# Attention's first unit in a hybrid encoder layer: late powers placed among the convolution's additions on GpSimd, head transposes through two PSUM banks, and TensorE's wait for the cleared row moved to the scores

## What is computed

```python
a = u[..., :C_CONV] * jax.nn.sigmoid(u[..., C_CONV:])          # 512 channels, 1024 tokens
a = lax.conv_general_dilated(a, conv_w[i], window_strides=(1,), # depthwise, 31 taps
                             padding=[(CONV_PAD, CONV_PAD)], ...) + conv_b[i]
a = jax.nn.silu(_layernorm(a, g_conv_ln[i], b_conv_ln[i]))

q = ((_rms(cq) * g_q_lat[i]) @ w_q_up[i]).reshape(B, S, N_HEADS, QK_HEAD)       # 8 heads of 96
kv = ((_rms(ckv) * g_kv_lat[i]) @ w_kv_up[i]).reshape(B, S, N_HEADS, QK_NOPE + V_HEAD)
...
q = _rms(q) * g_q_head[i]
k = _rms(k) * g_k_head[i]
...                                                             # rotary on 32 of the 96
att = _attention(q, k, v)                                       # full softmax, 1024 x 1024 a head
mix = jnp.concatenate([a, att], axis=-1) @ w_out[i]
```

## Time and profile before

| | |
|---|---|
| time, median of 3 runs | 1916.9 us |
| lowest and highest run | 1913.38 and 1918.84 us |
| the profiled execution's own time | 1915.36 us |
| its span, first to last instruction | 1913.4 us |
| PE busy | 1839.3 us, 96% |
| DVE, ACT, POOL busy | 1387.1, 798.3, 806.4 us |
| mean granted TensorE clock | 0.987 of full speed |

### The profile page before, as it was taken

The page is one execution under the profiler, slowest core; times in us unless marked ns, Lnnn a source line. Parts: engine busy times, 40 slices in busy tenths (PEclk is TensorE's granted clock), DMA queues, the critical chain, the costliest instruction groups (busy, mean ns, idle before and its releaser), DMA issues.

```text
span 1913.4 us, 22685 instructions
## 1 busy us (share of the span) xinstructions
PE 1839.3 (96%) x8039; PEld 1469.4 (77%) x8039; DVE 1387.1 (72%) x1776; ACT 798.3 (42%) x1255; POOL 806.4 (42%) x606
## 2 busy tenths in 40 slices
PE   4999999999999999997999999999999999999998
PEld 3788888888888878985656566877888888888886
DVE  6678888886777785766888886258656555677788
ACT  4532232223344554237676653154332333334444
POOL 1076655665200010019999952014566656620001
PEclk9999999999999999997999999999999999999999
DMA  9046666545763351000000024112333323466333
GB/s 352 13 142 192 215 213 210 194 154 194 253 214 94 114 183 56 17 1 0 1 1 0 0 64 156 66 56 83 110 111 110 105 89 110 171 231 242 100 106 130
DMA packets 132940, 232.12 MB, mean 121 GB/s; under 512 B 8796, under 2 KB 66243, under 8 KB 132578
## 3 DMA queue, kind: packets, MB, share of 16 engines
q1 hardware_dynamic: 132644, 230.73, 35.7%
q10 hardware_dynamic: 190, 0.01, 0.0%
HBM read 177.75 MB, written 52.95 MB: 121 GB/s over the span
## 4 chain that ended last, share of the span: by engine, by line
PE 36%; POOL 7%; issue 6%; DVE 5%; ACT 1%; DMA 1%; POOLq 0%; ACTq 0%; DVEq 0%
PE ps L508 19%; PE ps L862 9%; PE ps L2825 5%; POOL cv L1824 3%; POOL cv L1823 1%; PE ps L1665 1%; PE ps L382 1%; POOL slot L1774 1%; PE ps L1643 1%; DVE T L943 1%; POOL rqk L1759 0%; DVE ring L485 0%; POOL slot L1770 0%; POOL slot L1768 0%; POOL pp L1858 0%
## 5 line engine op out<-in xcount | busy, mean ns | idle before, releaser
L508 PE MATMUL ps<-T,ring 128*128 128x512 f32 x1920 | 441.8, 389 | 0.0
L508 PEld LDWEIGHTS ps<-T,ring 128*128 128x128 f32 x1920 | 360.3, 188 | 75.0 <-DVE ring L485 0.2
L508 PE MATMUL ps<-B,ring 128*128 128x512 f32 x1440 | 339.7, 392 | 4.4 <-DVE SG L567 3.6
L508 PEld LDWEIGHTS ps<-B,ring 128*128 128x128 f32 x1440 | 270.6, 189 | 64.2 <-issue 8.3
L574 POOL TENSOR_TENSOR HID<-HID,SG 128x512 f32<-128x512 f32 x80 | 122.1, 1527 | 262.9 <-DVE HID L559 152.1
L962 POOL TENSOR_SCALAR stat<-stat 128x1 f32<-128x1 f32 x31 | 12.0, 388 | 518.0 <-ACT XS L887 258.9
L862 PE MATMUL ps<-PW 128*128 128x512 f32 x924 | 217.3, 389 | 0.0
L862 PE MATMUL ps<-PT 128*128 128x512 f32 x900 | 212.1, 390 | 0.0
L862 PEld LDWEIGHTS ps<-PW 128*128 128x128 f32 x924 | 173.3, 188 | 36.1
L485 DVE TENSOR_TENSOR ring<-sums,ring 128x512 fp32r<-128x512 f32 x160 | 162.3, 1023 | 52.9 <-ACT ring L479 52.9
L862 PEld LDWEIGHTS ps<-PT 128*128 128x128 f32 x900 | 168.5, 188 | 34.8
(11 more groups left out here) (351 smaller groups left out, 3311.8 us busy)
## 6 DMA issues: line engine op xcount, KB each, us to landing
adat<-ffn_hidden SPq DMA_DIRECT2D x154, 256.0 KB, 2.7
ada_raw<-in_w_ada SPq DMA_DIRECT2D x56, 512.0 KB, 4.0
rawg<-in_ffn_wg SPq DMA_DIRECT2D x22, 1024.0 KB, 5.5
rawu<-in_ffn_wu SPq DMA_DIRECT2D x22, 1024.0 KB, 5.2
ffn_hidden<-HID SPq DMA_DIRECT2D x84, 256.0 KB, 2.9
ffn_hidden<-base SPq DMA_DIRECT2D x66, 256.0 KB, 3.0
H<-in_x SPq DMA_DIRECT2D x16, 512.0 KB, 6.4
h_saved_rows<-H SPq DMA_DIRECT2D x16, 512.0 KB, 2.6
```

Of the source, the lines that this page charges most:

```text
L508: mm = e.matmul(ps[:, product_bank(M, k)], ring[:, place % RING, wx, kc], RIGHT[k][:, xx, kc], start=(kc == 0 and i == 0), stop=(kc == HC ...
```

## The change

There are three edits. GpSimd's powers for the heads 2 to 7 of the three late tiles, which stood ahead of the convolution's first addition, are done one by one behind the additions 1, 2 and 3, and a wait for them stands ahead of the first slots that need them. The head units done in unit 0 use the banks `MISC` and 6 in turn, so that each transposition but the first waits for the low part of the unit before last. TensorE's wait for the cleared row is no longer ahead of unit 0 but ahead of its first scores.

```diff
-        def head_unit(n, first):
-
-            return (FIRST_HEAD[n], FIRST_BANKS[n]) if first else (n, MISC)
+        def head_unit(n, first, own_bank):
+
+            if first:
+                return FIRST_HEAD[n], FIRST_BANKS[n]
+            return n, (MISC, 6)[n % 2] if own_bank else MISC
 
         def pe_turn_head(e, i, hp, n, first=False):
-            u, bank = head_unit(n, first)
+            second = isinstance(i, int) and (i, hp) == (0, 1)
+            u, bank = head_unit(n, first, second)
...
                 e.wait_ge((slot_k, slot_q)[u // 2], i * 2 + (hp + 2))
-                e.wait_ge(qk_lo, i * 8 + (hp * 4 + n))
+                e.wait_ge(qk_lo, i * 8 + (hp * 4 + n) - (1 if second and n > 0 else 0))
...
-        def pool_late_inv_rms(e, a, b, done):
-            for t in range(LATE, NT):
-                r, ms, power = (of_heads(x, slice(t, t + 1), a, b)
-                                for x in (rqk, qs, mhalf[:].unsqueeze(1).broadcast_to([P, NT, 2 * NHD])))
-                e.tensor_tensor(r, ms, power, ALU.pow).then_inc(qk_rstd, 1)
-            e.wait_ge(qk_rstd, done + NT - LATE)
+        def pool_late_power(e, t, a, b):
+            r, ms, power = (of_heads(x, slice(t, t + 1), a, b)
+                            for x in (rqk, qs, mhalf[:].unsqueeze(1).broadcast_to([P, NT, 2 * NHD])))
+            e.tensor_tensor(r, ms, power, ALU.pow).then_inc(qk_rstd, 1)
...
             pool_first_slots(e)
-            pool_late_inv_rms(e, 1, 2, NT)
+            for t in range(LATE, NT):
+                pool_late_power(e, t, 1, 2)
+            e.wait_ge(qk_rstd, 2 * NT - LATE)
             pool_slots(e, 0, 1)
             e.wait_ge(slot_q, 3)
             e.memset(qkT[QK:AUG, :, :, LO].bitcast(F32), 0.0).then_inc(k_ones, 1)
             e.wait_ge(k_ones, 3)
-            pool_late_inv_rms(e, 2, NHD, 2 * NT - LATE)
             e.wait_ge(tap0, 2)
 
             def unit(i, m, first, last):
                 if m % NH == 1 and not last:
+                    if first and m == 1:
+                        e.wait_ge(qk_rstd, NT + 2 * (NT - LATE))
                     pool_slots(e, i + 1, m // NH)
                 if not last:
                     for n in products(m, 0, THALF):
                         pool_conv(e, i, n, first)
+                        if first and m == 0 and 1 <= n < 1 + NT - LATE:
+                            pool_late_power(e, LATE + n - 1, 2, NHD)
...
             pe_max_row(e, 0, 0, True)
-            e.wait_ge(k_ones, 3)
 
             def unit(i, m, first, last):
...
+                    if first and (m, p) == (0, 0):
+                        e.wait_ge(k_ones, 3)
                     pe_scores(e, i, m, p)
```

## The result

The changed kernel is slower. Its median is 1919.36 us (1914.02 to 1925.83, 22 runs) against 1915.25 us for the kernel before on the same chips (1911.41 to 1918.84, 22 runs): a ratio of 1.0023, 95% interval 1.0016 to 1.0030, so 3 to 6 us. The time itself lies at the upper edge of the range, 1913.2 to 1919.6; it does so by luck, since the range was made for scatter and two small rivals, and what happened is neither. The profiled execution took 1922.40 us, with a span of 1920.5 us, 7.1 us over before's.

The account below looks back on a forecast made before the run. TensorE was busy nearly throughout, with GpSimd also on the path from 919. TensorE's 2.3 us gain would be spent before unit 2 ends: net 0, within -0.2 and +0.2 us, so 1916.8 us, range 1913.2 to 1919.6.

Parts of the forecast that it names:

- two small rivals: GpSimd meets only one tap in unit 1: 1914.8 us, chance 0.15; a tap waits for power 3: 1918.1, chance 0.12.
- the moved wait: Unit 0's first transposition would then wait only for ScalarE's copy of the row of maxima; gain about 0.1 us.
- The banks: Head units in unit 0: removes TensorE's 1.34 us wait, but alone only moves the waiting to the next row of maxima.
- Addition 0: GpSimd in unit 0: starts at 887.7 rather than 894.51, no longer behind the three powers.
- ahead of addition 2: GpSimd in unit 0: now ahead of ScalarE, it waits 2.35 us for product 2, a wait not there before.
- TensorE's gap: Unit 0, ahead of the next row of maxima: still 2.7 us, so the low clock behind it stays likely.
- its gain there: TensorE's row of maxima in unit 0 at 902.4 rather than 904.66: 2.3 us, spent before unit 2 ends.
- The first tap: Unit 1's tap at about 904.8, inside power 3: meets a power and costs nothing.
- The last three meet slots and addition 6, 1.0 us each: Unit 1's taps at about 911, 914 and 917.6 lengthen GpSimd's operations, three meetings together 3.0 to 3.3 us.
- 37.5 to 37.8 us: GpSimd from 887.69 to addition 9: powers, additions, slots, wait and meetings summed, against 37.6 us before.
- five cases: GpSimd keeps the gain 0.15, tap meets a power 0.12, longer pattern 0.05, shorter pattern 0.04, forecast of no change 0.64.
- The rival for slower: Five half-turns from unit 2 to 1089: one more meeting each, 6.1 us slower in all, 1923 us; chance 0.05.

Follow-up runs that it names:

- own waits: Changed kernel with GpSimd waiting for its own last addition ahead of additions 5 to 9 and unit 1's slots: 1916.00 us; the same waits in powers alone: 1917.34 us.
- the powers alone: Only the three powers moved among the additions, banks and wait for the cleared row as before the change: 1924.85 us, ratio 1.0041 against the kernel before.
- the powers alone with memsets: Kernel with only the powers moved, plus four one-column VectorE memsets ahead of unit 1's tap of step 1: 1923.60 us, ratio 1.0042 against the kernel before.

## Why the prediction was wrong

**Right, step by step.** The transposition of head unit 0 gained nothing from the moved wait (0.77 us of waiting before and after, now put down to ScalarE's copy). The banks brought nothing (18.43 against 18.69 us). Addition 0 started at once, product 2 had no wait, GpSimd stood 2.68 us ahead of addition 2 (forecast 2.35), TensorE's gap was 2.82 us (2.7), and its gain there 1.9 us (2.3). The reading of the rows before had left out 0.70 us of waiting ahead of head unit 2 (895.89), which went too. The first tap met a power and paid nothing: 903.92 1.27 beside 903.62 2.28. By the Trainium skill (SBUF — State Buffer, Who interferes with whom) any GpSimd instruction that reads SBUF would have blocked it; the trace decides against that for the powers. Half-turns behind unit 2 kept their length.

**Wrong: the price of a meeting.** The step that failed is "The last three meet slots and addition 6, 1.0 us each", with its argument that "with GpSimd busy without a gap a tap can't miss it". The 1.0 us came from rows in which a tap had got in behind one operation, 920.55 among them. GpSimd had stood waiting 1.04 us just ahead of the addition that this tap met, and the forecast removed just such waits. The tap missed ten operations in a row and cost VectorE 11.5 us, which moved TensorE by 9.2 us in the profiled execution. The sum "37.5 to 37.8 us" up to addition 9 became 46.5 us. I had counted what a meeting costs GpSimd, which paces the stage, and taken VectorE's side, 1.1 us, as covered; held long enough, it is VectorE that the maxima and TensorE wait for.

**The sum itself, with holds taken away,** was about right: with own waits addition 9 stands at 41.60 us, before the change at 41.22 (0.4 later; the forecast, 0 within 0.2), and the output product 0.1 us from its old place; both differences are below the 1.35 us by which two profiles of nearly one kernel differ. Where the gain goes shows too. In that profile unit 2 starts 37.29 us from the memset where it started at 38.71, and unit 4 at 71.81 where it started at 70.77: units 2 and 3 take 34.5 us rather than 32.06. So the 1.4 us that TensorE still has at unit 2 are spent before unit 4, as the forecast said, and 1.0 us besides. None of the five cases named a hold over many operations. The rival for slower had another mechanism, a longer pattern in the later half-turns, which did not come (32.06 us and then 33.6, as before).

**What stays open.** Shown is that an operation with one SBUF input in the taps' place does not wait, that all long holds came in a queue without bubbles, and that 0.14 us bubbles end them. Not shown is why a tap gets in at other boundaries where no bubble shows in the timeline. A short unseen bubble from a wait that is met late can't be all of it, since some taps got in between the halves of an addition, where nothing is waited for. The kept profiles point elsewhere. Leave aside taps beside a power, and count GpSimd's operations since its last gap, or since the last one that was made longer by VectorE. In the first turn no tap with up to six of them behind it (7.6 us or less) was passed over by more than one further operation, and the five long holds had nine to eleven (11.9 to 14.7 us). One with eight (11.9 us) met a bubble and got in. The five held scalings of unit 2 had eleven or more. In the looped turns the same scaling got in at the next boundary with 13 or 14 (in the kernel before at 1004.88, behind 16 us without a gap). So in code that is not looped the length of the undisturbed stretch sorts the cases as well as the bubbles do. No run varied it by itself, and what lies behind it, and what the loop changes, is open.

## What to carry to other kernels

An engine's idle time can be a service to another. Before filling GpSimd's waits with work, list VectorE's operations with two SBUF inputs in that stretch and what is queued behind them, and price a meeting from rows with the same neighbours: a price taken next to gaps says nothing of a queue without them. If such a queue is wanted, let GpSimd wait for its own last operation now and then (0.14 us each), or stand an operation beside which the other engine passes (here a power) where the other asks.

## What the runs showed that was not expected

- A VectorE operation with two SBUF inputs can be passed over by ten GpSimd operations in a row: 12.74, 13.95 and 13.91 us for one of 1.28 us, until GpSimd had nothing released. The Trainium skill (SBUF — State Buffer, Who interferes with whom) has the later one blocked until the first finishes; here it was not let in between.
- GpSimd's power on 128x12 (2.28 us) and VectorE's tap don't hinder each other, though both read SBUF: 1.27 us beside it, in the changed kernel and with the powers alone.
- Four one-column VectorE memsets ahead of a tap delay it by about 0.03 us together.
- The times of the powers alone fall into two groups (1916 to 1918 and 1925 to 1926 us, one run between). The length of the hold explains only part of such a spread: the changed kernel's two profiles, with taps of 12.74 and 6.27 us, took 1922.40 and 1917.22 us, but the powers alone with memsets took 1919.95 us with a tap of 13.91, and with own waits 1920.50 us with no tap over 1.74.
